# Two transformer blocks on one core: another order around four passages and in the second block's attentions

## The reference

```python
def reference(x, mem, ...):
    x = first_block(x, mem, ...)     # 512 tokens of 1024 values, 256 memory rows
    return second_block(x, ...)

def first_block(...):
    h = rms_norm(x, g[0]); proj = h @ w_in
    ...   # hyena, neighbourhood attention, short convolution, gated and merged
    x = x + rms_norm(merged @ w_out, g[1])
    x = x + rms_norm(memory_cross_attention(rms_norm(x, g[2]), mem_n, wq, wkv, wo), g[3])
    x = x + rms_norm(conv_glu_ffn(rms_norm(x, g[4]), w_up, w_conv, w_down), g[5])

def memory_cross_attention(h, mem_n, wq, wkv, wo):      # 4 heads of 256
    p = softmax(q @ km.T * XA_HEAD_DIM ** -0.5)
    return (p @ vm).reshape(B, L, D_MODEL) @ wo

def second_block(...):
    proj = rms_norm_2(h, attn_norm) @ w_in
    y_a = mla_mixer(...)     # 6 heads, latent attention, rotated parts
    y_b = diff_mixer(...)    # 4 heads, p[:, 0] - lam * p[:, 1]
    y_c = swa_mixer(...)     # 6 heads, window of 128, sinks
    h = h + concatenate([y_a, y_b, y_c]) @ w_out
    h = h + (silu(hn @ w_gate) * (hn @ w_up)) @ w_down
    return rms_norm_2(h, final_norm)[:, META_BLK:]
```

## Time and profile before

| | us |
|---|---|
| median of three runs | 1954.23 (1951.95 to 1955.97) |
| profiled execution | 1953.56 |
| its span | 1951.8 |
| mean granted clock of TensorE | 0.965 |
| TensorE busy | 1829.9 (94%) |
| its weight loads, beside it | 1464.6 (75%) |
| VectorE busy | 1011.5 (52%) |
| ScalarE busy | 733.3 (38%) |
| POOL busy | 289.3 (15%) |

### The profile page before, as it was taken

The page is one execution under the profiler, slowest core; times in us unless marked ns, Lnnn a source line. Parts: engine busy times, 40 slices in busy tenths (PEclk is TensorE's granted clock), DMA queues, the critical chain, the costliest instruction groups (busy, mean ns, idle before and its releaser), DMA issues. The chain is left out here.

```text
span 1951.8 us, 22257 instructions
## 1 busy us (share of the span) xinstructions
PE 1829.9 (94%) x8987; PEld 1464.6 (75%) x8987; DVE 1011.5 (52%) x1517; ACT 733.3 (38%) x1219; POOL 289.3 (15%) x233
## 2 busy tenths in 40 slices
PE   7899999999999978989999999889878989999998
PEld 5678877788888766868888788877655768888887
DVE  6777844444444455358777522674454534444322
ACT  4433344333334433334444322444445533322221
POOL 1023500111102130141111100500100011111000
PEclk9999999999999989989999999898877989999999
DMA  5222322132224320222222222321200122222221
GB/s 185 87 86 87 106 79 76 65 121 95 97 98 164 117 75 33 76 76 87 86 97 97 87 98 87 119 81 68 88 22 32 44 75 88 97 97 97 87 97 54
DMA packets 49829, 171.13 MB, mean 88 GB/s; under 512 B 5882, under 2 KB 8570, under 8 KB 49600
## 3 DMA queue, kind: packets, MB, share of 16 engines
q1 hardware_dynamic: 45216, 155.69, 23.1%
q0 software_dynamic: 3936, 13.51, 2.0%
q10 hardware_dynamic: 576, 0.52, 0.1%
HBM read 165.51 MB, written 4.19 MB: 87 GB/s over the span
## 5 line engine op out<-in xcount | busy, mean ns | idle before, releaser
L308 DVE TENSOR_TENSOR ws_l<-raw,ws_h 128x1024 fp32r<-128x1024 f32 x289 | 387.9, 1346 | 574.3 <-ACT ws_h L300 573.9
L371 PE MATMUL ps<-h_h,ws_h 128*128 128x512 f32 (+1 forms) x1448 | 584.8, 404 | 38.9 <-DVE ws_l L308 13.3
L372 PE MATMUL ps<-h_l,ws_h 128*128 128x512 f32 (+1 forms) x1448 | 572.9, 396 | 0.0
L373 PE MATMUL ps<-h_h,ws_l 128*128 128x512 f32 (+1 forms) x1448 | 571.7, 395 | 0.0
L300 ACT ACTIVATE ws_h<-raw 128x1024 fp32r<-128x1024 f32 x289 | 303.6, 1054 | 490.4 <-PE ps L373 486.8
L371 PEld LDWEIGHTS ps<-h_h,ws_h 128*128 128x128 f32 x1448 | 278.4, 192 | 115.2 <-issue 29.1
L373 PEld LDWEIGHTS ps<-h_h,ws_l 128*128 128x128 f32 x1448 | 278.7, 192 | 62.1
L372 PEld LDWEIGHTS ps<-h_l,ws_h 128*128 128x128 f32 x1448 | 279.2, 193 | 58.4 <-issue 0.2
L371 PE MATMUL ps<-G_h,ws_h 128*128 128x512 f32 (+1 forms) x374 | 143.5, 384 | 4.2 <-DVE ws_l L308 4.2
L372 PE MATMUL ps<-G_l,ws_h 128*128 128x512 f32 (+1 forms) x374 | 143.3, 383 | 0.0
L373 PE MATMUL ps<-G_h,ws_l 128*128 128x512 f32 (+1 forms) x374 | 143.3, 383 | 0.0
(11 more groups left out here) (438 smaller groups left out, 2429.9 us busy)
## 6 DMA issues: line engine op xcount, KB each, us to landing
raw<-in_ffn_up SPq DMA_DIRECT2D x88, 512.0 KB, 3.2
raw<-in_w_merge SPq DMA_DIRECT2D x36, 512.0 KB, 3.2
raw<-in_ffn_down SPq DMA_DIRECT2D x22, 512.0 KB, 3.2
raw<-in_w_down SPq DMA_DIRECT2D x22, 512.0 KB, 3.2
raw<-in_w_hy SPq DMA_DIRECT2D x12, 512.0 KB, 4.8
raw<-in_w_sc SPq DMA_DIRECT2D x12, 512.0 KB, 3.3
raw<-in_fwd SPq DMA_DIRECT2D x8, 512.0 KB, 3.2
raw<-in_w_naqk SPq DMA_DIRECT2D x8, 512.0 KB, 3.2
```

What stands on the lines that cost most here:

```text
L308: dve.e.tensor_tensor(w.lo, raw[n % NRAW][:], w.hi, ALU.subtract).then_inc(*lo_made.says(("lo", n)))
L371: pe.e.matmul(o, a.hi, b.hi, start=start, stop=False, skip_group_check=True)
L372: pe.e.matmul(o, a.hi, b.lo, start=False, stop=False, skip_group_check=True)
L373: return pe.e.matmul(o, a.lo, b.hi, start=False, stop=stop, skip_group_check=True)
```

## The change

1. In the first residual passage the splits `beside(m)` stand on VectorE behind the tile's multiply instead of ahead of it, for m = 1, 2, 3, 5 instead of 1, 3, 5 (the fourth came after the passage), and the query tiles take banks from a ring of their own.
2. In the cross attention each block of 128 rows of P is scaled by itself as soon as its exponentials are there, and TensorE turns P with the identity.
3. The spread of the FFN norms comes behind tile (2, 1) instead of (2, 0).
4. In the first FFN the first split call of the down projection comes before the last round of the up projection's.
5. In the attentions ScalarE takes the steps in the order of `copies_first`: exponentials wait in `held` until the copies of the unit's turn are issued. The splits there run one chunk ahead instead of two (`lead`). The difference has one instruction less.
6. The out projection of the attentions takes parts in another order (`LAST_PARTS`), and its splits are spread between squares and h pieces.

```diff
-LAST_PARTS = [(m, k) for m in range(7) for k in (5, 6)] + [(m, 7) for m in range(7)] + [(7, k) for k in (5, 6, 7)]
+LAST_PARTS = [(m, k) for m in range(3) for k in (5, 6)] + [(m, 7) for m in range(3)] + [
+    (m, k) for m in range(3, 8) for k in (5, 6, 7)]
...
+    lead = {"n": NSPLIT}
...
-        while m < n + NSPLIT and (m < NSPLIT or over_at.get(m - NSPLIT, n + 1) <= n):
+        while m < n + lead["n"] and (m < NSPLIT or over_at.get(m - NSPLIT, n + 1) <= n):
...
         for m in range(8):
-            beside(m)
             i, old = rings["dve T"].take(("rs", v, m))
...
             if m > 1:
                 h_rest(nv, m - 2, ngain, dst(m - 2))
+            beside(m)
...
+    XA_BESIDE = (1, 2, 3, 5)
...
+        xq_banks = Ring(place, [bank_at["k", 7], bank_at["v2", 0, 0], bank_at["v2", 0, 1], bank_at["r1", 6], bank_at["r1", 7]])
...
-            for kc in range(2):
-                b = bank(("xt", hd, kc), ring)
-                pe.wait_ge(("xa diag", hd))
-                for j in range(4):
-                    i = mm32(b[:, 128 * j:128 * j + 128], xaP[z][:, j, kc * 128:(kc + 1) * 128],
-                             xaD[z][:, 128 * j:128 * j + 128])
-                i.then_inc(*products.says(("done", ("xt", hd, kc)), ("xa diag used", hd)))
-                yield
+            b = [bank(("xt", hd, kc), ring) for kc in range(2)]
+            for j in range(4):
+                pe.wait_ge(("xa over", hd, j))
+                for kc in range(2):
+                    i = pe.e.transpose(b[kc][:, 128 * j:128 * j + 128], xaP[z][:, j, kc * 128:(kc + 1) * 128], ident[:])
...
-        residual_act("r1", "n2", "ng2", hm, chunk_act, lambda m: chunk_act() if m in (1, 3, 5) else None)
+        residual_act("r1", "n2", "ng2", hm, chunk_act, lambda m: chunk_act() if m in XA_BESIDE else None)
...
+            def scaled(j):
+
+                dve.wait_ge(("xP", hd, j))
+                dve.e.reciprocal(s[:, 12 + j:13 + j], s[:, 8 + j:9 + j]).then_inc(*dve_part.says(("xover", hd, j)))
+                dve.wait_ge(("xover", hd, j))
+                dve.e.tensor_scalar(xaP[z][:, j, :], xaP[z][:, j, :], s[:, 12 + j:13 + j], None, ALU.mult).then_inc(
+                    *dve_part.says(("xa over", hd, j)))
...
-                elif (i, j) == (2, 0):
+                elif (i, j) == (2, 1):
                     spread_tokens(v, bank(("spread", v), rings["seven"]))
...
+        down = Follow(chunk_act)
         for n in range(23):
             f.next(8 if n == 0 else 16 if n < 22 else 0)
+            if n == 22:
+                down.next(8)
...
     def out2_act():
+        lead["n"] = NSPLIT
...
-        f.next(24)
...
+        f.next(8)
+        for m in range(7):
+            squared_x(m)
+            if m < 5:
+                begun(m)
+            if m in (1, 4):
+                f.next(8)
+        for m in range(5, 8):
+            begun(m)
+        rings["f"].next(8)
+        load_roots()
+        squared_x(7)
...
+    def copies_first():
+
+        held = []
+        for step in ORDER:
+            if step[0] == "scores":
+                held.append(step)
+                continue
+            if step[0] in ("turn", "turned"):
+                n = at_unit[step[1]] + (step[0] == "turned") * len(LINE)
+                yield from (s for s in held if at_unit[s[1]] <= n)
+                held = [s for s in held if at_unit[s[1]] > n]
+            yield step
+
     def attention_act():
+        lead["n"] = 2
...
-        for what, u, c in ORDER:
+        for what, u, c in copies_first():
...
             dve.e.reciprocal(s, numbers(u, 6)).then_inc(*dve_part.says(("dif 0", u)))
-            dve.wait_ge(("dif 0", u))
-            dve.e.tensor_tensor(s, s, s0, ALU.mult).then_inc(*dve_part.says(("dif 1", u)))
-            dve.wait_ge(("dif 1", u), "lam")
-            dve.e.tensor_scalar(s, s, LAM, -1.0, ALU.mult, ALU.mult).then_inc(*dve_part.says(("dif 2", u)))
+            dve.wait_ge(("dif 0", u), "lam")
+            dve.e.scalar_tensor_tensor(s, s, LAM, s0, ALU.mult, ALU.mult).then_inc(*dve_part.says(("dif 2", u)))
```

More of the change, by code:

```diff
@@ L1486, in xa_pe @@
         for m in (3, 4):
-            tile(bank(("xq", m), main), blocks, 8, hk, ("xq", m), lambda k: ("h", "n2", k))
+            tile(bank(("xq", m), xq_banks), blocks, 8, hk, ("xq", m), lambda k: ("h", "n2", k))
             if m == 3:
@@ L1570, in xa_act @@
         for m in range(5):
[L1571 removed]
+            if m:
+                f.next(8)
             if m == 3:
@@ L1684, in attend @@
                     *dve_part.says(("xneg", hd, j)))
+                if j:
+                    scaled(j - 1)
                 yield
             yield
-            dve.wait_ge(("xP", hd, 3))
-            dve.e.reciprocal(s[:, 12:16], s[:, 8:12]).then_inc(*dve_part.says(("xover", hd)))
-            dve.wait_ge(("xover", hd), ("xa diag used", hd - 2) if hd > 1 else ("off done", "r1"))
-            for j in range(4):
-                dve.e.tensor_scalar(xaD[z][:, 128 * j:128 * j + 128], ident[:], s[:, 12 + j:13 + j], None,
-                                    ALU.mult).then_inc(*dve_part.says(("xa diag", hd)))
+            scaled(3)
             yield
@@ L1777, in ffn1_act @@
         rings["act T"] = Ring(place, (3, 4, 5), ("G1", 21))
-        f = Follow(chunk_act)
         for m in range(8):
-            f.next(22)
+            down.next(22 if m else 14)
             outputs_act("r5", m, "n4")
@@ L1811, in ffn1_dve @@
         rings["dve T"] = Ring(place, (0, 1, 2), ("G1", 21))
-        f = Follow(chunk_dve)
         for m in range(8):
-            f.next(22)
+            down.next(22 if m else 14)
     def ffn1_pool():
```

43 lines of the change are left out of this document (25 added, 18 removed).

## The result

The changed kernel took 1927.09 us, the median of four runs (1922.39 to 1930.18); the kernel before, run beside it, 1954.15 (1951.95 to 1955.97). The ratio is 0.986, with a 95% interval of 0.9836 to 0.9883, so about 27 us less. The forecast was 1917, with a range of 1900 to 1936 that holds it: the direction was right, and the gain about three quarters of what was expected. The profiled execution has a span of 1928.4 us and a mean clock of 0.967 (before 1951.8 and 0.965).

The account below looks back on a forecast made before the run. TensorE's order of work plus 122 us of standing and lower clock bound the kernel. Terms (a) to (f) summed to 37.1 us, taken from 1953.56: 1916.5, against the median 1917; range 1900 to 1936.

Parts of the forecast that it names:

- (a): First residual to cross attention: waits of 4.8 us in place of 14.8, perhaps 1.5 us of clock; gain 11.5 us.
- (e): Passage out of the attentions: third up chunk's low part split earlier, ahead of squares and h pieces; gain 1.5 us.
- rival 1: Attentions: waits go from copies to exponentials, (f) gives 0 to 4, time 1927; chance 0.28 together with rival 2.
- rival 2: Whole kernel: halved waits keep the half clock, (a) to (f) lose about 10 us, 1927; chance 0.28 with rival 1.
- No transfer holds it: Whole kernel: no transfer holds TensorE, as the raw weight chunks land well before use; no size given.
- (b): Cross attention heads: 32 transposes replace 64 half-products, chain shorter, heads 2 and 3 slower; gain 4.0 us, ends 1 and 5.5.
- (c): FFN norm spread one tile later: the 2.64 us wait goes; gain 4.1 us in second FFN, 0 in first.
- (d): First FFN, third down-projection chunk split earlier: 3.03 us wait goes with 1.2 us of clock; gain 4.0 us.
- (f): Attentions: copies 8.7, clock 5, shorter difference 0.8, h_l waits −2.5, shorter lead costs nothing; gain 12 us.
- The fifth: Gains of (a), (c), (d) hidden by a later late step: (a) 5, the rest half, time 1931; chance 0.10.
- The fourth: Attentions: each next turn waits for its four exponentials, 51 us in and 13.7 out, time 1966; chance 0.02.

Follow-up runs that it names:

- the later sum: The changed kernel with the token sum of the cross attention's norm one query tile later, its spread behind tile 4: 1927.47 us, ratio 0.9889.

## Why the prediction was right or wrong

The time lies in the range, but the gain is 10 us short of the forecast, and the parts missed it both ways: (a) lost 6.5 us of it and the banks 2.5, (e) brought 3.4 more. That the total lands at 1927, the number of rivals 1 and 2, is chance: rival 1's shift of the waits came only in small, and rival 2's clock was missing in (a) more than in the attentions.

**Bounds.** The reading of the profile held: TensorE's stream with its waits, and half clock behind many of them, though not behind each. "No transfer holds it" has one exception, the start of the kernel before:

```profile
PE ps L376 <- DMA KA<-in_w: 7.3, 1, 7.3
```

**(a) Passage, 11.5 expected, about 5 measured.** The chain was followed rightly as far as the waits go: 4.8 us of them expected, 5.7 measured, one on the second chunk (2.0 expected, 2.57 measured) and one on POOL's sums (1.6 and 2.90; the adds had a median of 1.66 us and not 1.43). VectorE was busy 8.3 of 10.7 us beside them, 4.4 of 10.3 before; that this slowed them is not shown. The range given for their end was too narrow as well: six adds at the 2.18 of the row would end at 704.0, not at 700.9. The step that failed is the last, "and perhaps 1.5 us of clock". 2.3 us did come back at the old wait, but the new wait put 7 us of half clock, 3.4 us lost, where there was none, and other stretches came with it. This is the largest miss, and it is a term that was mis-sized, with the low end of 8 not low enough.

**(b) Heads, 4.0 expected, 2 to 4 measured.** The stage with the new heads is 120.2 us in the first profile and 118.1 to 119.5 in others, against 122.5 with the old heads behind the same passage. The products that turn P take 5.3 us in place of 9.2, so 3.9 us went against 4.2 expected, and the one wait on the diagonals, 3.34 us, is 2.06. The 128x256 multiply took 0.353 us, 0.30 expected between the rows, and 0.19 by the Trainium skill's page "VectorE: DVE Perf Modes", section "The TRN2 errata — SBUF-src ops pay a fixed extra latency per instruction": as with the 128x512 row, the measured time is above what that formula gives. The price that was foreseen in heads 2 and 3, 2.3 to 2.5 us, did not come as a wait: TensorE waits 1.1 and 1.0 us there for the scaled rows, and waited 0.4 and 1.8 us for the diagonals. What took its place is clock, 3.4 or 6.8 us at half speed from 769 or 771 us on (the old heads behind the new passage have 3.4 of it too), so the number came out for another reason.

The changed kernel, line L1691 (minimum, median, maximum in ns, then the shapes):

```profile
L1691 DVE TENSOR_SCALAR xaP<-xaP,xast x16: 352/353/356, 728.5 to 770.4; 128x256 f32<-128x256 f32 x16
```

**(c) Spread, 4.1 and 0 expected, 4.1 and −1.3 to −3 measured.** The second FFN is exact. In the first the mechanism came as told, the wait goes and comes back at the pair of splits, but longer than the one it replaced. The step that failed there is "some 2 to 3 us against the chunk": it counted how much later the splits come and left out that TensorE itself comes earlier, by the wait it no longer has. One profile is inside the end of +2, the other outside.

**(d) Down chunk, 4.0 expected, 4.7 measured**: the 3.03 us and the whole 1.7 of clock.

**(e) Passage out, 1.5 expected, 4.9 measured.** The wait at the third up chunk went from 3.92 to 2.21 and its 6.8 us of half clock with it; I had counted on a new wait for what the split passes, which did not come. The clock in it is luck: three variants kept 3.4 us of it and gained 3.3 to 3.5.

**(f) Attentions, 12 expected, 10.4 and 10.7 measured**, up to 15 in variants with the same attention code. The parts: copies 8.7 expected, 10.0 measured on the two lines that it counted and 11.5 with all waits on copies; the longer wait for h_l −2.5 expected for two places, −2.2 and −1.4 measured at two; idle time in all 6.2 less; the clock the rest, 4, against 5. Of the 6.2, 2 us are only moved: the wait for the first exponentials gave way to the one for `QN_l`, ahead of the stage. The size of the longer wait for h_l held, its reason did not: at 1408.59 the split is held by the exponentials on ScalarE itself and not by VectorE's difference. The shorter difference (0.8 expected) shows where the order is the old one: its two waits are 7.1 us before, 6.5 with the lead alone, and 5.9 with both; in the changed kernel they are 7.1 again.

**Not in the sum:** the banks, −2.5 to −2.7 at the way in, and −2.2 us ahead of the first residual norm, where no instruction was changed. The first is a real omission: the diff showed five tiles leaving the ring of seven, and I looked only at who waits for the banks they now take, not at who gets the banks that they no longer take. The order shows no bank, so it has to be worked out from the ring.

**Rivals.** The fifth had (a) at 5, as it came, but (c) and (d) were not halved by it; its own terms add up to 26.5 us and 1928, not 1931. The fourth, exponentials in place of copies at every turn, did not come; TensorE waits 0.9 us for P in the stage, in two waits. The first came in small, at two difference units. The second, the clock does not come back, is what (a) suffered; for the attentions it is neither right nor wrong: the stage's mean clock is 0.86, between the 0.87 named for the forecast and the 0.85 named for this rival, and 72 us at half speed became 61, 51 with the later sum and 79 with the old lead. The section "A second HAM failure mode: psum-queue depth-cycling" of the Trainium skill's page "TensorE: Matmul & The Clock Gate" had many small idles keep the clock switching, and the trace agrees that it switches as often as before with the copy waits shortened: nine stretches at 0.50 between 1303 and 1495 us, where before had eight.

## What to carry to other kernels

A wait that is taken away pays twice only if no other takes its place near by: before a gain in clock is counted, find the next late thing and put its own half clock on the other side. When a tile leaves a ring of buffers, every later user of the ring changes its buffer; either keep the phase or check who owned the buffer that each critical tile now gets. Where two engines walk one list, holding one kind of step on one of them also holds all that stands behind it there, and what the other engine makes of that.

## What the runs showed of the hardware

The same code, with nearly the same waits, can run at half clock for different lengths. Ahead of the first residual norm no instruction differs between the two kernels. TensorE's long waits there differ by at most 0.6 us each, and all its waits sum to less in the slower profile (27.4 us against 28.6). And yet the stage took 665.73 us in one profile, 667.88 in another, 665.27 to 667.92 over all fourteen. Two windows there, first of the changed kernel's first profile, then of before (columns as in the earlier trace rows):

```profile
54.50:57.50 3.00, 3.00 (x9) 2.33 (x8) 2.71 (x4) 1.11 (x2) 0.00 (x0) 0.50 0.35 119
334.50:337.50 3.00, 3.00 (x12) 1.85 (x11) 1.80 (x2) 0.80 (x1) 0.00 (x0) 0.52 0.00 0
```

```profile
54.50:57.50 3.00, 3.00 (x14) 2.43 (x13) 2.67 (x5) 1.03 (x2) 0.00 (x0) 1.00 0.22 71
334.50:337.50 3.00, 3.00 (x17) 2.17 (x16) 2.21 (x7) 1.27 (x5) 0.00 (x0) 1.00 0.18 42
```

Two waits of 2.38 us (at 52.56) and 1.86 us (at 332.50) were followed by half clock in one execution and not in the other. A longer wait does it too. The 3.03 us wait at the first down chunk was followed by 3.4 us at half clock in the kernel before and by none with the copies alone put into it, where it is 3.03 us as well:

```profile
1110.60:1114.00 3.40, 3.40 (x15) 2.76 (x16) 2.21 (x2) 0.58 (x1) 0.00 (x0) 1.00 0.63 183
```

In the attentions the same instruction list gave 217.96 to 222.54 us; where all that comes ahead of it was the same too, three profiles agreed within 0.4 us (222.54, 222.22, 222.20), so a shift of the stage against what came before seems to matter more than chance there. A wait of 2 to 4 us has no fixed price in clock, and that may be a part of the width of the single runs of before, 1941 to 1963 us. What lets one execution keep its clock is not shown here.
